# Expert layer: 32 tokens of a dense block take their key values by dots on fetched rows, and the first dense product has 352 columns

## The reference, cut to what matters

```python
def peer(xn, wq, keys, u, v):            # xn: (512 tokens, 1024)
    def block(xb):
        q = (xb @ wq).reshape(PEER_BLOCK, PEER_HEADS, 2, PEER_DKEY // 2)
        s1 = jnp.einsum('thd,hnd->thn', q[:, :, 0], keys[:, 0]).astype(f32)
        s2 = jnp.einsum('thd,hnd->thn', q[:, :, 1], keys[:, 1]).astype(f32)
        v1, i1 = lax.top_k(s1, PEER_TOPK)
        v2, i2 = lax.top_k(s2, PEER_TOPK)
        cand = (v1[..., :, None] + v2[..., None, :]).reshape(...)
        sc, ci = lax.top_k(cand, PEER_TOPK)
        e = (take(i1, ci // PEER_TOPK) * PEER_NKEYS + take(i2, ci % PEER_TOPK))
        g = jax.nn.softmax(sc, axis=-1)
        hid = jnp.einsum('thkd,td->thk', u[e], xb).astype(f32)
        a = (jax.nn.gelu(hid, approximate=False) * g).astype(xb.dtype)
        return jnp.einsum('thk,thkd->td', a, v[e])
```

## Time and profile before

| | |
|---|---|
| three runs | 3084.8, 3085.78, 3086.91 us |
| profiled execution, its span | 3086.42 us, 3084.6 us |
| TensorE busy | 3052.7 us, 99% |
| TensorE weight load busy | 2583.5 us, 84% |
| VectorE, ScalarE, GpSimd busy | 60%, 37%, 62% |
| hidden stage (units 0 to 127) | from 1910.9 to 2551.4 us of the span |

### The profile page before, as it was taken

How to read it: one execution, slowest core, us unless ns; L and a number is a source line. 1 busy time by engine, 2 the same in 40 slices (tenths; PEclk the granted TensorE clock), 3 DMA queues, 4 the chain that set the end, 5 groups by cost and what they waited for, 6 DMA issues and landing times.

```text
span 3084.6 us, 42480 instructions
## 1 busy us (share of the span) xinstructions
PE 3052.7 (99%) x15287; PEld 2583.5 (84%) x15287; DVE 1844.3 (60%) x3299; ACT 1150.3 (37%) x2065; POOL 1904.1 (62%) x1796
## 2 busy tenths in 40 slices
PE   8999999999999999999999999999999999999999
PEld 7877788888668888888777888999999998888887
DVE  7674544316856442250673236679878868877886
ACT  3455222102553221120554212434357763333333
POOL 7422666677337666776443576578875566766663
PEclk9999999999999999999999999999999999999999
DMA  7110222222212222222112222478888899999995
GB/s 236 69 42 28 103 96 96 96 96 103 76 42 103 96 96 96 96 103 96 69 55 76 81 95 96 173 283 299 300 315 318 325 347 372 368 367 361 360 364 203
DMA packets 154430, 539.26 MB, mean 175 GB/s; under 512 B 11364, under 2 KB 64773, under 8 KB 118021
## 3 DMA queue, kind: packets, MB, share of 16 engines
q1 hardware_dynamic: 98916, 338.80, 30.8%
q0 software_dynamic: 36864, 134.23, 11.9%
q10 hardware_dynamic: 18464, 63.70, 5.4%
HBM read 479.16 MB, written 57.40 MB: 174 GB/s over the span
## 4 chain that ended last, share of the span: by engine, by line
PE 97%; DVE 1%; ACT 1%; issue 0%; DMA 0%; ACTq 0%; DVEq 0%
PE banks L194 85%; PE banks L2879 3%; PE banks L2217 1%; PE banks L2255 1%; PE banks L1131 1%; PE banks L1200 1%; PE banks L1218 1%; PE banks L1190 1%; PE banks L2234 1%; PE banks L2823 1%; PE banks L1778 0%; PE banks L1816 0%; PE banks L1794 0%; PE banks L1738 0%; PE banks L495 0%
## 5 line engine op out<-in xcount | busy, mean ns | idle before, releaser
L194 PE MATMUL banks<-memory,weights_split 128*128 128x512 f32 (+1 forms) x9456 | 2066.0, 375 | 12.7 <-DVE memory L577 8.9
L194 PEld LDWEIGHTS banks<-memory,weights_split 128*128 128x128 f32 x9456 | 1714.1, 188 | 285.3 <-issue 34.8
L3503 POOL TENSOR_SCALAR weights_split<-weights_raw 128x512 fp32r<-128x512 f32 x576 | 377.1, 664 | 773.3 <-issue 384.0
L3508 POOL TENSOR_TENSOR weights_split<-weights_raw,weights_split 128x512 fp32r<-128x512 f32 x576 | 768.2, 1346 | 0.2
L3348 POOL TENSOR_TENSOR weights_split<-weights_raw,weights_split 128x512 fp32r<-128x512 f32 x384 | 507.7, 1346 | 303.2 <-ACT weights_split L3173 302.2
L194 PE MATMUL banks<-weights_split,memory 128*128 128x512 f32 (+1 forms) x2880 | 646.4, 386 | 0.0
L194 PEld LDWEIGHTS banks<-weights_split,memory 128*128 128x128 f32 x2880 | 533.8, 188 | 108.8 <-issue 1.0
L3173 ACT ACTIVATE weights_split<-weights_raw 128x1024 fp32r<-128x1024 f32 x256 | 269.4, 1053 | 82.8 <-DMA weights_raw<-in_weights 46.5
L711 DVE TENSOR_TENSOR banks<-banks,memory 128x512 f32<-128x512 f32 x88 | 61.3, 699 | 231.9 <-PE banks L194 231.8
L2951 DVE CUSTOM_DVE_ANT_0 memory<-memory,banks 128x1024 f32<-128x1024 f32 x128 | 154.7, 1210 | 68.3 <-DMA memory<-in_peer_u,memory 68.1
L3342 POOL DMA_INDIRECT memory<-in_peer_v,memory x128 | 157.3, 1229 | 43.5 <-issue 24.5
(11 more groups left out here) (284 smaller groups left out, 2721.5 us busy)
## 6 DMA issues: line engine op xcount, KB each, us to landing
weights_raw<-in_weights SPq DMA_DIRECT2D x271, 1024.0 KB, 4.9
routing<-memory ACTq DMA_DIRECT2D x12, 2048.0 KB, 11.6
hidden<-memory ACTq DMA_DIRECT2D x62, 384.0 KB, 5.5
memory<-hidden SPq DMA_DIRECT2D x31, 768.0 KB, 13.3
memory<-routing SPq DMA_DIRECT2D x30, 768.0 KB, 10.4
window_rows<-memory ACTq DMA_DIRECT2D x1, 3064.0 KB, 25.3
chunk_rows<-memory ACTq DMA_DIRECT2D x1, 2556.0 KB, 11.0
memory<-window_rows ACTq DMA_DIRECT2D x8, 256.0 KB, 3.4
```

The costliest lines, as they stand in the source:

```text
L194: last = k.nc.tensor.matmul(out, left[a], right[b], start=start and n == 0, stop=stop and n == 2, skip_group_check=True)
L3503: k.nc.gpsimd.tensor_scalar(cut(high, n * PIECE, PIECE), cut(raw, n * PIECE, PIECE), 1.0, 1.0, ALU.mult, ALU.mult).then_inc(k.high_made, 1)
L3508: k.nc.gpsimd.tensor_tensor(cut(low, n * PIECE, PIECE), cut(raw, n * PIECE, PIECE), cut(high, n * PIECE, PIECE).bitcast(F32), ALU.subtract ...
```

## The change

Of the third dense block the last 32 tokens (`PICKED`) leave the first dense product: `hidden(n)` now has 352 columns (`WIDE`). The places of these 32 tokens in the hidden buffers hold ones. Their key values are dots instead: 32 tokens times 128 wanted rows are 4096 dots, which is 32 fetches and 32 dots of 128 partitions, each partition holding one of the 32 tokens, four groups of wanted rows for each. The results pass Gelu and multiply the tokens' shares before the matrix is built. The value product keeps 384 columns.

- Fetches and dots go from 128 to 160 for key rows; the value rows stay 128 (`ROWS` is 288). Dots 58 to 89 are the new ones. They read `picked_tokens`, which is `gathered[-1]`, a buffer in SBUF; the other dots go on reading `tokens` in PSUM.
- The block with the 32 tokens is routed second. Its expert numbers are spread by a matmul and picked out on VectorE (`take_numbers`), its token vectors are summed (`sum_picked`), turned (`turn_picked`, behind unit 54) and copied.
- Dots per route go from 22 to 31, placed by a table of the steps' times; 55 instead of 50 stand among the one-hot rows. The matrix starts behind unit 89 instead of 85. The operand of the product lies contiguous instead of in three pieces.
- `fetch` starts behind the low half of unit 14 instead of 21.

```diff
     lists = 2 * PEER_HEADS
-    ORDER = [DENSE_BLOCKS] + list(range(DENSE_BLOCKS))
+    ORDER = [DENSE_BLOCKS, DENSE_BLOCKS - 1] + list(range(DENSE_BLOCKS - 1))
     RESULT_ORDER = [DENSE_BLOCKS] + list(range(DENSE_BLOCKS))
-    DOTS = P
-    SCORE_AT, EXP_AT, TURN_AT = [0, 8, 27, 50], [15, 38, 60, 82], [None, 45, 67, 84]
-    MATRIX_FIRST, MATRIX_COUNT = 85, 34
-    IN_ROUTE, IN_MATRIX, BEFORE_GATES = [0, 22, 22, 22], 50, 12
+    PICKED, GROUPS = 32, P // 32
+    WIDE, FIRST_PICKED = DENSE - PICKED, P - PICKED
+    DOTS = P + PICKED
+    ROWS = DOTS + P
+    SCORE_AT, EXP_AT, TURN_AT = [0, 8, 21, 48], [11, 34, 57, 82], [None, 43, 67, 88]
+    MATRIX_FIRST, MATRIX_COUNT = 89, 34
+    IN_ROUTE, IN_MATRIX, BEFORE_GATES = [0, 31, 31, 31], 55, 12
+    PICKED_AT, NUMBERS_AT, SUMS_AT, TOKENS_AT, FACTORS_AT = 58, 46, 52, 54, 86
+    STEP_TIMES = [32, 116, 148, 193, 201, 224, 252, 315, 343, 375, 378, 382, 405, 428, 451, 474, 497, 520]
     SPARSE_END = 123
 
     def planned(unit):
 
 
-        marks = [(19, 0), (42, 22), (64, 44), (84, 66), (118, 116), (125, DOTS), (PEER_KEYS + 3, DOTS),
-                 (PEER_KEYS + SPARSE_END, 2 * DOTS)]
+        marks = [(10, 0), (36, 31), (59, 62), (84, 93), (122, 148), (126, DOTS), (PEER_KEYS + 3, DOTS),
+                 (PEER_KEYS + SPARSE_END, ROWS)]
         if unit <= marks[0][0]:
             return 0
         for (u0, c0), (u1, c1) in zip(marks, marks[1:]):
             if unit <= u1:
                 return c0 + (c1 - c0) * (unit - u0) // (u1 - u0)
         return marks[-1][1]
+
+    def job(i):
+
+        if i >= DOTS:
+            return "value", i - DOTS
+        if PICKED_AT <= i < PICKED_AT + PICKED:
+            return "picked", i - PICKED_AT
+        return "sparse", i if i < PICKED_AT else i - PICKED
 
...
-    gathered += of_block[0:DENSE_BLOCKS]
+    gathered += [of_block[b] for b in ORDER[1:]]
+    picked_tokens = gathered[-1]
...
     homes = []
-    for i in range(2 * DOTS):
+    for i in range(ROWS):
         if i < DOTS:
-            homes.append(ASKED[i % (6 if i < 12 else 7 if i < 33 else 8 if i < 112 else len(ALWAYS))])
+            last_picked = PICKED_AT + PICKED
+            homes.append(ASKED[i % (6 if i < 20 else 7 if i < last_picked else 8 if i < DOTS - 16 else len(ALWAYS))])
...
-                begun, last = split_product(k, by_block(cut(bank.memory, 0, DENSE)),
+                begun, last = split_product(k, cut(bank.memory, 0, WIDE),
                                             k.tile(unit_place(n)[0], n % 2 * D_TILES + kk),
-                                            [hn_tile(side, kk)[:, 0:DENSE_BLOCKS] for side in range(2)], kk == 0, kk == D_TILES - 1)
+                                            [hn_dense(side, kk, WIDE) for side in range(2)], kk == 0, kk == D_TILES - 1)
                 if kk == 0:
...
+        def turn_picked():
+            pe.wait_ge(copied, 4 * BLOCKS)
+            pe.wait_ge(picked_summed, 1)
+            for n in range(D_TILES):
+                last = mm(score_banks[n // 4].memory[:, n % 4 * P:(n % 4 + 1) * P],
+                          cut(picked_tokens, n * P, P), k.const("ident"), start=True, stop=True,
+                          skip_group_check=True)
+            last.then_inc(picked_turned, 1)
+
+        def spread_numbers():
+            pe.wait_ge(masks_made, 3)
+            pe.wait_ge(numbered, 1)
+            mm(score_banks[0].memory[:, 3 * P:4 * P], chooser, all_numbers, start=True,
+               stop=True, skip_group_check=True)
+
+        def turn_factors():
+            pe.wait_ge(factors_placed, 1)
+            mm(score_banks[1].memory[:, 0:PICKED], placed, token_mask, start=True, stop=True,
+               skip_group_check=True).then_inc(factors_turned, 1)
 
         def turn_choices(r):
             pe.wait_ge(copied, 4 * min(r + 2, BLOCKS))
             pe.wait_ge(chosen_ready, r + 1)
             if r >= 2:
                 pe.wait_ge(emptied, 3 * (r - 1))
+            if r == 1:
+                spread_numbers()
+            if r == 2:
+                pe.wait_ge(picked_kept, 2)
+            if r == BLOCKS - 1:
+                turn_factors()
...
             else:
                 pe.wait_ge(emptied, 3 * DENSE_BLOCKS)
+                pe.wait_ge(picked_weighed, 1)
...
         v = k.nc.vector
-        j = i % DOTS
+        kind, j = job(i)
         row = gathered[homes[i]]
         dve.wait_ge(row_in[homes[i]], 16 * uses[i])
         if i == 0:
             dve.wait_ge(tokens_turned, 1)
-        if i < DOTS:
-            v.tensor_tensor_reduce(out=row, in0=row, in1=tokens, scale=1.0, scalar=0.0, op0=ALU.mult, op1=ALU.add,
-                                   accum_out=cut(hid, j, 1)).then_inc(eaten, 1)
+        if i == PICKED_AT:
+            dve.wait_ge(picked_kept, 2)
+        if kind != "value":
+            of, to = (tokens, hid) if kind == "sparse" else (picked_tokens, picked_hid)
+            v.tensor_tensor_reduce(out=row, in0=row, in1=of, scale=1.0, scalar=0.0, op0=ALU.mult, op1=ALU.add,
+                                   accum_out=cut(to, j, 1)).then_inc(eaten, 1)
...
             for _ in range(count):
+                if sparse_done[0] == NUMBERS_AT:
+                    take_numbers()
+                if sparse_done[0] == SUMS_AT:
+                    sum_picked()
                 sparse(dve, sparse_done[0])
                 sparse_done[0] += 1
+
+        def sum_picked():
+            dve.wait_ge(k.x_low, hn.made_before + D_TILES)
+            dve.wait_ge(scored, 2 * BLOCKS)
+            v.tensor_tensor(picked_tokens.rearrange("p (n q t) -> p n q t", q=GROUPS, t=PICKED),
+                            *(cut(hn.memory, side * D_TILES * TOKENS, D_TILES * DENSE).rearrange(
+                                "p (n t) -> p n t", t=DENSE)[:, :, WIDE:DENSE].bitcast(F32).unsqueeze(2).broadcast_to(
+                                    [P, D_TILES, GROUPS, PICKED]) for side in range(2)),
+                            ALU.add).then_inc(picked_summed, 1)
+
...
+        def take_numbers():
+            dve.wait_ge(spread_copied, 1)
+            dve.wait_ge(masks_made, 3)
+            v.tensor_tensor(by_group(spread), by_group(spread), of_group(group_mask), ALU.mult).then_inc(numbers_made, 1)
+            dve.wait_ge(numbers_made, 1)
+            v.tensor_reduce(picked_hid, spread.rearrange("p (q j) -> p j q", j=PICKED), AX.X, ALU.add).then_inc(numbers_made, 1)
+            dve.wait_ge(numbers_made, 2)
+            v.tensor_copy(numbers.bitcast(U32), picked_hid).then_inc(numbers_made, 1)
+            dve.wait_ge(numbers_made, 3)
+
+        def place_factors():
+            dve.wait_ge(factors_made, 1)
+            v.tensor_tensor(by_group(placed), picked_factor.unsqueeze(1).broadcast_to([P, GROUPS, PICKED]),
+                            of_group(group_mask), ALU.mult).then_inc(factors_placed, 1)
+
+        def weigh_picked():
+            dve.wait_ge(factors_turned, 1)
+            dve.wait_ge(emptied, 6)
+            shares_picked = cut(turned, 2 * DENSE + WIDE, PICKED)
+            v.tensor_tensor(shares_picked, shares_picked, score_banks[1].memory[:, 0:PICKED],
+                            ALU.mult).then_inc(picked_weighed, 1)
 
...
-                if left[0] > 2 and (r > 1 or step[0] > 1):
-                    consume(1)
-                    left[0] -= 1
+                if counting[0] and step[0] <= len(STEP_TIMES):
+                    goal = IN_ROUTE[r] * STEP_TIMES[step[0] - 1] // STEP_TIMES[-1]
+                    count = max(0, goal - (IN_ROUTE[r] - left[0])) if r > 1 or step[0] > 1 else 0
+                    consume(count)
...
+            if r == 1:
+                v.scalar_tensor_tensor(out=all_numbers, in0=chosen[:, 0:P], scalar=float(PEER_KEYS), in1=chosen[:, P:2 * P],
+                                       op0=ALU.mult, op1=ALU.add).then_inc(numbered, 1)
...
-            a.activation(buffer[:, n % 2 * DENSE:(n % 2 + 1) * DENSE], cut(bank.memory, 0, DENSE),
-                         ACT.Gelu).then_inc(activated, 1)
+            a.activation(cut(buffer, n % 2 * DENSE, WIDE), cut(bank.memory, 0, WIDE), ACT.Gelu).then_inc(activated, 1)
...
+            if n == TOKENS_AT:
+                act.wait_ge(picked_turned, 1)
+                for half in range(2):
+                    a.activation(picked_tokens[:, half * 512:(half + 1) * 512], score_banks[half].memory,
+                                 ACT.Copy).then_inc(picked_kept, 1)
+            if n == FACTORS_AT:
+                act.wait_ge(eaten, PICKED_AT + PICKED)
+                a.activation(picked_factor, picked_hid, ACT.Gelu).then_inc(factors_made, 1)
...
+            kind, j = job(i)
+            if i == PICKED_AT:
+                pool.wait_ge(numbers_made, 3)
             table = k.dram["peer_u"] if i < DOTS else k.dram["peer_v"]
-            j = i % DOTS
+            of = numbers if kind == "picked" else expert
             k.nc.gpsimd.indirect_dma_start(
                 gathered[home], None, table,
```

(8 more changed lines are left out.)

67 lines of the change are left out of this document (52 added, 15 removed).

## The result

The changed kernel takes 3108.15 us (median of four runs, 3103.26 to 3111.35) against 3085.77 in the same session: ratio 1.0072, 95% interval 1.0060 to 1.0084. It is 22.4 us slower. The forecast was 3091, its range 3054 to 3110, and slower had the largest chance, 0.42. The profiled execution took 3106.93 us, its span 3105.1.

A forecast was written before the change was run, and what follows sets the result against it. TensorE was taken as the bound, with GpSimd close beside it. Terms -39.6 + 2.5 + 4 + 24 + 6 + 7 = +3.9 us gave 3089.7, raised to 3091 because stalls feed each other; range 3054 to 3110.

The forecast's parts named there:

- The columns: First dense product: 32 of 384 columns removed in 3072 matmuls, 160.9 ns each, saving 39.6 us (37.2 to 40.6).
- the added matmuls: On TensorE, `turn_picked` and two single matmuls for the picked tokens add 2.5 us together.
- the fourth rival: Weight load bounds matmuls below 384 columns, so no column is saved: 3093, chance 0.04.
- The new dots: Units 60 to 85: picked dots with two SBUF operands and GpSimd exclude each other; TensorE stalls 24 us (0 to 35).
- GpSimd's 105%: Units 57 to 81: GpSimd needs 101.8 us for weights and 33 fetches against TensorE's 96.8; before, 88%.
- its lead of 6.7 us: GpSimd has low halves ready 6.7 us before TensorE needs them, which alone would cover the 5 us of excess.
- The rival without exclusion: Picked dots do not exclude GpSimd, so the 24 us and part of the matrix start go: 3063, chance 0.25.
- The first fetches: Near unit 15: five earlier fetches delay its low half and meet the next weights on the DMAs; 4 us (0 to 9).
- The start and stage of the matrix: Scaling waits behind a split with late weights, 4 us, plus 2 inside the 34 matrix units; 6 us (0 to 12).
- The change to the value stage: Last key row is fetched later, so dots and gate come late, with DMAs full; 7 us (0 to 14).
- The rival of full DMAs: From unit 36 to 84 and in the matrix stage the DMAs become the bound: 3110, chance 0.18.

The follow-up runs named there:

- e1: Changed kernel with its 32 picked dots reading the tokens in PSUM instead of the copy in SBUF; 3094.47 us, ratio 1.0024.
- e5: Kernel before, 384 columns, with 32 of its 128 dots reading an SBUF operand instead of the tokens in PSUM; 3087.25 us, ratio 1.0005.
- e12: Changed kernel without picked fetches and dots, at the old pace (22 dots a route, fetches from unit 19), token sum behind dot 30; 3063.61 us.
- e8: Changed kernel without the 32 picked fetches, each picked dot replaced by a write of one column; 3088.49 us, ratio 1.0000.
- e4: Changed kernel with the first dense product kept at 384 columns, all additions present; 3112.81 us, ratio 1.0093.
- e3: Kernel before with 348 instead of 384 columns in the first dense product, no picked tokens; 3054.97 us, ratio 0.9905.
- e9: Changed kernel with the fetch plan held at 93 rows from unit 84 to unit 87; 3101.70 us, ratio 1.0051.
- e2: Changed kernel with each of the 32 picked fetches bringing 128 elements of a row instead of 1024; 3108.72 us, ratio 1.0082.
- e7: Changed kernel without the 32 picked fetches, picked dots reading the tokens in PSUM; 3088.37 us, ratio 1.0003.

## Why the prediction was right about the sign and 17 us short

**The columns** and **the added matmuls** came as worked out: where nothing disturbs them, 24 matmuls of 352 columns last 3.84 to 3.87 us, 160 to 161 ns; the weight load does not bound them, so the fourth rival falls.

**The new dots** were the right mechanism, about the right size in the trace (19.3 us in units 54 to 88 against 24), and rightly found from rows of another stage. Taken alone it is 14.8 us (e1): the rest of the stretch is the fetches, 6.5, which I had counted in GpSimd's 105% but let its lead of 6.7 us cover. The rule of the Trainium skill that I quoted ("SBUF — State Buffer", section "SBUF: two separate sides") is now borne out for the dot's own instruction: 1191 to 1226 ns with one operand in PSUM, up to 3603 with both in SBUF (e1 against the changed kernel). The rival without exclusion (3063) falls. Its price is not in the rule: 1.5 us in e5, 14.8 here. One detail I had otherwise: I let a dot wait for one low piece and the next piece wait for the dot. The longest dots let both pieces of a pair pass (last section).

**The first fetches** are the step that failed, together with the matrix stage below. I priced the earlier start as one meeting of five fetches with unit 15, 4 us, and took it that TensorE's queue has no other gap before unit 60. That meeting cost about 2 us (TensorE waited 0.38 and 1.31 us there). But the trace has 14.6 us in units 9 to 54, and e12 against e8 gives the denser plan, with what it does at the matrix, 22.5 us. In these traces neither the denser plan nor the shorter unit does it alone. The stretch from 1960 to 2110 us of e4 (the dense plan, 384 columns), of e3 (the old plan, 348 columns) and of the changed kernel (columns as in the earlier trace rows):

```profile
1960.00:2110.00 150.00, 150.00 (x875) 149.26 (x875) 135.16 (x433) 60.61 (x84) 129.30 (x113) 1.00 0.88 313
```

```profile
1960.00:2110.00 150.00, 149.96 (x955) 148.84 (x954) 113.95 (x401) 64.28 (x89) 123.51 (x105) 1.00 0.80 280
```

```profile
1960.00:2110.00 150.00, 144.85 (x886) 141.60 (x885) 132.65 (x436) 57.99 (x83) 128.45 (x112) 0.99 0.89 310
```

With both, e1 and e9 have 141.7 and 141.8 us of TensorE there. One trace stands apart: e12, old plan and 352 columns, has 143.76 in its slowest execution, 10 us above its median.

I had worked out GpSimd's time per unit only for units 57 to 81. The same sum for units 14 to 39, behind which 36 fetches stand, is 26 x 3.67 + 10 x 1.26 = 108 us against TensorE's 104 (26 x 3.86 and two halves of `score`). It would have shown most of the lead of 6.7 us going, but not yet a stall. For that I would have had to watch a second engine: the late weights reach TensorE by ScalarE too, whose copies of the scores stand behind the split.

**The start and stage of the matrix** (6) measured 16.8. The wait before the first matrix matmul is the one I named, scaling behind a split that waits for weights, 6.5 us for 4. The 10.3 us inside the stage are the whole saving of its 34 units, for which I had 2. Rows of the changed kernel's GpSimd there:

```profile
2315.31 0.95 POOL L3479 DMA_INDIRECT memory<-in_peer_u,memory  x1 [3.70 <-DVE memory L3016]
...
2319.44 0.94 POOL L3479 DMA_INDIRECT memory<-in_peer_u,memory  x1 [3.18 <-DVE memory L3016]
...
2325.10 0.95 POOL L3479 DMA_INDIRECT memory<-in_peer_u,memory  x1 [2.18 <-DVE memory L3016]
```

At unit 90, behind the first matrix, the plan asks for 103 rows, and the last of them takes the buffer of the dot with number 94 (from 0), while VectorE enters the matrix with 93 done. (The expectation of e9 has 102 at unit 89; counted again it is 101 there.) The old plan asked for 70 rows at unit 86, which need dot 61, with 66 done; e9's asks for 99 at unit 90, which need dot 90. All of this could be read from the numbers of the diff. e9 takes it away and the saving comes. The wait in front of the matrix is not the plan's alone: e12's trace has it too, 5.04 us, behind weights that ScalarE got 4.18 us late.

**The change to the value stage**: 4.5 us for 7, the mechanism as told (last key row fetched at 2563.30, its dot begun at 2571.97, the gate at 2573.12). The 2 us inside the value stage I did not foresee, and no run separates them.

**The rival of full DMAs** named 3110 and the time is 3108, but for another reason in the units it named: with the bytes of the picked rows cut to an eighth (e2) the time stays. That 3108 lies inside the range is therefore luck: its upper end was drawn for this rival, and two terms were short by 10 us each. What remains of the rival is latency: weight loads take longer to land where units are shorter (5.1, 8.2 and 9.0 us in the kernel before, e3 and e1, at DMA shares of 0.83, 0.88 and 0.93 from 2110 to 2300 us), and the stage has two slots for them. How much of the 22.5 us of the pace is that, and how much GpSimd's and ScalarE's queues, no run separates.

In short, from the kernel before: columns with all preparation -22.5 (e12), the plan's pace +22.5 (e8), dots +0.9 (e7), their fetches +6.5 (e1), the exclusion +14.8: +22.2. Each step carries some 5 us of uncertainty; by the medians they are -22.2, +24.5, -0.1, +6.8 and +13.4.

## What to carry to other kernels

When a change shortens the unit of the bounding engine, work out for every stretch of the stage what each in-order queue does in one unit, and not only where the new work stands: here the busiest stretch was found and the plan around it, changed by a few numbers, cost as much. A fetch that may wait for a free buffer must not stand in front of work that the bounding engine needs; compare the plan's count at each stage border with the buffers and the consumer's count. And an exclusion costs what the slack beside it leaves: 32 such dots cost 1.5 us where most of them met matrix units of 6.7 us (e5), and 14.8 where all met units of 3.86 us with the added fetches; with those fetches but units of 4.17 us, TensorE's waits for low halves in that stretch were 7.0 us instead of 12.8 (e4).
